# Adding the expert outputs back: four-pass fp32 products with weighted selections, against one-pass products with plain selections and a two-part expert output

## The chip, the cores and the metric

The kernel runs on one core of a Trainium2 chip. Its time is the device time of one execution in microseconds (us); of several executions the median is given. The engines named below are TensorE (PE in the profile, its weight loads PEld), VectorE (DVE), ScalarE (ACT), GpSimd (POOL) and SyncE (SP), which issues nearly all DMAs.

## The reference, cut to what matters

A trunk of two layers over 256 frames of width 1024. Its last part is a mixture of eight experts, of which each frame takes two:

```python
logits = xt.astype(F32) @ w_router.astype(F32)
top_logit, top_idx = lax.top_k(logits, TOP_K)            # TOP_K = 2
gates = jax.nn.softmax(top_logit, axis=-1).reshape(-1)
...
def expert_block(args):
    tok, e = args
    xb = xt[tok]
    return (jax.nn.silu(xb @ w_gate[e]) * (xb @ w_up[e])) @ w_down[e]
...
contrib = y_rows[pos].astype(F32) * gates[:, None]
y = jax.ops.segment_sum(contrib, flat_tok, num_segments=n_tok)
```

What this case is about is the last two lines: each frame gets the rows of its two experts, each times its gate, and this is added to the residual x.

## The kernel before

The first 620 us or so are the two mixers, the dense SwiGLU and the router. After them comes one pass per *item*. An item is one expert with 96 slots for rows (3 groups of 32, `NG` = 3, `GRP` = 32); items 0 to 7 are the eight experts, and up to five more would be run by a loop with a register if an expert had over 96 rows. Each engine has its own program, written out in the order in which it runs; semaphores tie them together (`filled(use)`: TensorE has filled a PSUM bank; `drained(use)`: it has been read).

TensorE's order in an item (`expert_item`, line 1277) is `EXPERT_ORDER`: the first 2048 columns of gate (8 pieces) and up (8), the other 1536 columns of gate and up, then 14 pieces of down. Every piece is a DMA of 1024 KB or 768 KB into a ring that holds 14 of the large ones; SP issues the next one as soon as the piece that lay in its place has been used. The gate, up and down products are plain fp32 on *column* tiles: four products of 32 output rows each, side by side (lines 1203 and 1224). One fp32 product in the code makes two weight loads and two MATMULs in the trace; a product of fp32r operands makes one of each.

The expert's output (32 slots of a group, times 4 quarters `q` of 256 columns, over the 128 partitions) ends in three banks `("md", r)`, numbers 2, 6 and 7. ScalarE copies each to `y_e` (line 1575), and that copy drains the bank.

`one_hot` (VectorE, L1963) writes for each frame and slot whether the frame's row lies in it, times the frame's gate; TensorE turns this over (`turned_selection`, L1239) and ScalarE copies it to `sgt` (L1568). `combine(item)` (L1272) then makes, for each of two frame tiles `t`, three groups `r` and four quarters `q`, one fp32 product of 32 rows with 128 frames and 256 columns: 24 products on *row* tiles, the four quarters in four different row groups of the array, into four banks `("mc", q)`, numbers 3 to 6. VectorE adds these to x, 128x512 at a time (`add_contributions`, L2126), which drains them.

`combine(item - 1)` stands inside the next item, behind gate pieces 0 and 1; seven of the eight stand so. The eighth is the kernel's last work on TensorE, behind the loop with the register, and is followed by `add_contributions`, the final norm and the output.

In the trace `expert_rows` is the memory of `y_e`, `m_silu` and `m_act`, and `arena` that of the selections, `sgt` and the gathered rows.

Of the kernel before, what the change touches and what calls it, by code (L numbers as in the profile page):

```python
# [27 lines left out]
F32 = mybir.dt.float32  # L28
F32R = mybir.dt.float32r
I32 = mybir.dt.int32  # L30
ALU = mybir.AluOpType
ACT = mybir.ActivationFunctionType
AX = mybir.AxisListType.X

P = 128
SEQ = 256
T = SEQ // P
DM = 1024
DK = DM // P
# [8 lines left out]
D_FF = 7 * DM // 2  # L48
FC = 512
NCH = D_FF // FC  # L50
NE = 8
GRP = 32
NG = 3
SLOTS = NG * GRP
NQ = P // GRP
# [193 lines left out]
DN = DM // NQ  # L249
DOWN_ORDER = (2, 0, 1)  # L250
# [100 lines left out]
def build_trunk(nc, x_d, w, cst_d, out_d):  # L351
    uses, bank_fills_per_item, bank_signals_per_item = plan_banks()

    with ExitStack() as ctx:
# [3 lines left out]
        def sem(name):  # L358
            return ctx.enter_context(nc.semaphore(name))
# [12 lines left out]
        def ps(use):  # L372
            return bank[uses[use][0]][:, :]
# [9 lines left out]
        def fill_sem(use):  # L383
            return s_filled[uses[use][0]]

        def drain_sem(use):
            return s_drained[uses[use][0]]

        def open_bank(pe, use, item=0):

            b, n, _ = uses[use]
            if n > 1:
                pe.wait_ge(s_drained[b], n - 1 + item * bank_fills_per_item[b])
# [11 lines left out]
        x = sb("x", [P, T, DM])  # L405
# [45 lines left out]
        def layout(region, *parts):  # L451
            at, out = 0, []
            for shape in parts:
                out.append(view(region, at, *shape))
                at += int(np.prod(shape))
            taken[0] = max(taken[0], at)
            return out
# [14 lines left out]
        ml_h = hn[:, :, 0:512]  # L472
        ml_o = hn[:, :, 512:1024]

        xg_all, xg, m_act_t, sel, sel_q, sgt = layout(
            arena, (NE, DK, SLOTS), (DK, SLOTS), (NG, D_FF // P, GRP), (T, SLOTS), (T, NQ * SLOTS), (NG, SEQ))
        assert taken[0] <= ARENA and T * NE * SLOTS <= NG * D_FF // P * GRP

        xt, xt_parts, w_router = layout(arena, (T, DK, P), (T, P), (DK, GRP))  # L480
        m_silu, m_act, y_e = layout(expert_rows, (NG, 512), (NG, 512), (NG, DN))

        taken[0] = 0
# [79 lines left out]
        rsel_ready = sem("rsel_ready")  # L564
        route_ready = sem("route_ready")
        sel_ready = sem("sel_ready")
        experts_done = sem("experts_done")
        out_ready = sem("out_ready")
        out_done = sem("out_done")
# [209 lines left out]
        def _(pe):  # L779
# [479 lines left out]
            def combine(item):  # L1259

                for r in DOWN_ORDER:
                    pe.wait_ge(*drained(("md", r), item))
                for half in range(2):
                    pe.wait_ge(*drained(("sgt", half), item))
                for t in range(T):
                    for r in range(NG):
                        for q in range(NQ):
                            use = ("mc", q)
                            if t == 0 and r == 0:
                                open_bank(pe, use, item)  # L1270
                            rows = slice(q * GRP, (q + 1) * GRP)
                            last = mm(ps(use)[:, t * DN:(t + 1) * DN], sgt[rows, r, t * P:(t + 1) * P], y_e[rows, r, :],  # L1272
                                      start=r == 0, stop=r == NG - 1)
                            if t == T - 1 and r == NG - 1:
                                last.then_inc(fill_sem(use), 1)

            def expert_item(item, first=False):

# [56 lines left out]
        def _(act):  # L1335
# [223 lines left out]
            def expert_item(item, first=False):  # L1559
                if first:  # L1560
                    for half, k in FIRST_ROWS:
                        gathered_rows(half, k)
                gate_silu(0, item)
                for half in range(2):
                    use = ("sgt", half)
                    act.wait_ge(*filled(use, item))
                    rows = 2 - half
                    fn(sgt[:, 2 * half:2 * half + rows, :],  # L1568
                       ps(use)[:, 0:rows * SEQ].rearrange("p (r c) -> p r c", r=rows), ACT.Copy).then_inc(
                           drain_sem(use), 1)  # L1570
                gate_silu(1, item)
                for r in DOWN_ORDER:
                    use = ("md", r)
                    act.wait_ge(*filled(use, item))
                    fn(y_e[:, r, :], ps(use)[:, 0:DN], ACT.Copy).then_inc(drain_sem(use), 1)  # L1575

            for item in range(NE):
                expert_item(item, item == 0)
# [64 lines left out]
        def _(dve):  # L1643
# [314 lines left out]
            def one_hot(item):  # L1958

                for t in range(T):  # L1960
                    pos = pos_i[:, bass.ds(item, 1), t]
                    slot = cst[:, C_IOTA:C_IOTA + SLOTS].rearrange("p (r s) -> p r s", r=NG)
                    last = V.tensor_scalar(sel_q[:, t, :].rearrange("p (r q s) -> p r q s", r=NG, q=NQ),  # L1963
                                           slot[:, :, None, :].to_broadcast([P, NG, NQ, GRP]), pos,
                                           gate_i[:, bass.ds(item, 1), t], ALU.is_equal, ALU.mult)
                last.then_inc(sel_ready, 1)

            def one_hot_extra(item):
# [134 lines left out]
            def gated(part, item):  # L2103

                width, first = WIDTHS[part], PARTS[part][0] // P
                blocks = width // GRP
                for r in range(NG):
                    use = ("mu", part, r)
                    dve.wait_ge(*drained(("mg", part, r), item))
                    dve.wait_ge(*filled(use, item))  # L2110
                    if part:
                        dve.wait_ge(turned_ready, 2 * NG * item + r + 1)
                    V.tensor_tensor(m_act[:, r, 0:width], m_silu[:, r, 0:width], ps(use)[:, 0:width],  # L2113
                                    ALU.mult).then_inc(drain_sem(use), 1)
                for r in range(NG):
                    dve.wait_ge(*drained(("mu", part, r), item))
                    V.transpose(m_act_t[:, r, first:first + blocks, :].rearrange("p b c -> p (b c)"),
                                m_act[:, r, 0:width]).then_inc(turned_ready, 1)

            def add_contributions(item):  # L2120

                for q in range(NQ):
                    use = ("mc", q)
                    cols = x[:, :, q * DN:(q + 1) * DN]
                    dve.wait_ge(*filled(use, item))
                    V.tensor_tensor(cols, cols, ps(use).rearrange("p (t c) -> p t c", t=T), ALU.add).then_inc(  # L2126
                        drain_sem(use), 1)

            def expert_item(item, first=False):
                if not first:  # L2130
                    add_contributions(item - 1)
                    for half in range(2):
                        dve.wait_ge(*filled(("sgt", half), item - 1))
                one_hot(item)
                gated(0, item)
                gated(1, item)

            def rows_extra(item):

# [45 lines left out]
```

## Time and profile before

| | us |
|---|---|
| three runs of the kernel before | 1520.58, 1522.92, 1525.62 (median 1522.92) |
| the profiled execution | 1522.43 |
| its span in the trace | 1520.6 |
| PE busy | 1458.4 (96% of the span) |
| PEld busy | 892.3 (59%) |
| DVE busy | 410.4 (27%) |
| ACT busy | 328.8 (22%) |
| mean DMA rate over the span | 288 GB/s |

Busy time is what an engine's instructions cover. The chain of waits is read back from the last instruction to what released each step, so that it shows the work that set the end. A windows view gives busy time and the number of instructions that touch each stretch (x), and the granted clock of TensorE (1.00 is 2.4 GHz, 0.50 is 1.2 GHz). Matmuls overlap: the mean of one (from its start to its end) is longer than the distance between two starts.

### The profile page before, as it was taken

The numbers are of one execution on the slowest core, as the hardware profiler recorded it, in microseconds if no ns is written. First come the engines' busy times: TensorE is split into PE (matmuls) and PEld (weight loads), VectorE is DVE, ScalarE is ACT, GpSimd is POOL, SyncE is SP. The second block draws the span as 40 slices with busy tenths as digits, with TensorE's granted clock in tenths as the row PEclk, the third lists the DMA queues.
The fourth block names the chain that finished last, engine by engine and source line by source line (L and its number), as shares of the span: only waits on it lengthen the run. The fifth ranks groups of instructions, "written<-read, shape, count | busy, mean of one in ns | idle before, by whom it ended". The sixth has DMA issues, their size and how long they took to land.

```text
span 1520.6 us, 34140 instructions
## 1 busy us (share of the span) xinstructions
PE 1458.4 (96%) x15653; PEld 892.3 (59%) x15653; DVE 410.4 (27%) x638; ACT 328.8 (22%) x479; POOL 24.5 (2%) x43
## 2 busy tenths in 40 slices
PE   4999899999999979999999999999999999999995
PEld 3986799999798965345345345344344354354353
DVE  3454654444565753300100100100100100000101
ACT  4332544434538642100000000000000000000001
POOL 2000000000001100000000000000000000000000
PEclk9999999999999999999999999999999999999997
DMA  9530555555444328999999999999999999999960
GB/s 308 176 111 28 176 173 191 189 175 191 139 143 149 111 84 318 333 410 403 376 400 400 381 395 399 387 397 391 387 401 389 386 404 392 387 400 392 387 247 29
DMA packets 132600, 438.51 MB, mean 288 GB/s; under 512 B 10626, under 2 KB 63968, under 8 KB 116064
## 3 DMA queue, kind: packets, MB, share of 16 engines
q1 hardware_dynamic: 131232, 432.73, 75.4%
q0 software_dynamic: 1216, 3.51, 0.8%
q8 instruction: 125, 2.05, 0.5%
q14 instruction: 27, 0.22, 0.0%
HBM read 435.16 MB, written 1.05 MB: 287 GB/s over the span
## 4 chain that ended last, share of the span: by engine, by line
PE 93%; DVE 2%; ACT 2%; issue 1%; DMA 1%; SPq 1%; POOL 0%; DVEq 0%; ACTq 0%
PE bank L1203 38%; PE bank L1224 19%; PE bank L799 9%; PE bank L800 9%; PE bank L801 9%; PE bank L1272 2%; ACT high L627 1%; PE bank L1254 1%; PE bank L899 1%; DMA raw<-in_ev_w_in 1%; DVE low L632 1%; PE bank L1239 1%; SPq L740 0%; PE bank L918 0%; PE bank L917 0%
## 5 line engine op out<-in xcount | busy, mean ns | idle before, releaser
L1203 PE MATMUL bank<-ring,arena 128*32 128x512 f32 (+1 forms) x6144 | 585.9, 540 | 0.0
L1203 PEld LDWEIGHTS bank<-ring,arena 128*32 128x32 f32 x6144 | 196.5, 110 | 365.3 <-issue 364.1
L1224 PE MATMUL bank<-ring,arena 128*32 128x256 f32 x5376 | 291.5, 379 | 0.0
L1224 PEld LDWEIGHTS bank<-ring,arena 128*32 128x32 f32 x5376 | 174.7, 110 | 117.1 <-issue 3.1
L632 DVE TENSOR_TENSOR low<-raw,high 128x2048 fp32r<-128x2048 f32 x74 | 169.2, 2290 | 174.7 <-ACT high L627 174.7
L799 PE MATMUL bank<-ht_h,high 128*128 128x256 f32 x672 | 193.7, 288 | 4.0 <-DVE vec L1741 3.0
L800 PE MATMUL bank<-ht_l,high 128*128 128x256 f32 x672 | 192.2, 286 | 0.0
L801 PE MATMUL bank<-ht_h,low 128*128 128x256 f32 x672 | 192.0, 286 | 0.0
L627 ACT ACTIVATE high<-raw 128x2048 fp32r<-128x2048 f32 x74 | 141.6, 1913 | 162.9 <-PE bank L801 159.1
L2113 DVE TENSOR_TENSOR expert_rows<-expert_rows,bank 128x512 f32<-128x512 f32 (+1 forms) x48 | 29.7, 621 | 469.8 <-PE bank L1203 251.2
L799 PEld LDWEIGHTS bank<-ht_h,high 128*128 128x128 f32 x672 | 131.2, 195 | 5.7 <-issue 5.1
L800 PEld LDWEIGHTS bank<-ht_l,high 128*128 128x128 f32 x672 | 131.1, 195 | 0.2
L801 PEld LDWEIGHTS bank<-ht_h,low 128*128 128x128 f32 x672 | 131.1, 195 | 0.0
L2126 DVE TENSOR_TENSOR x<-x,bank 128x512 f32<-128x512 f32 x32 | 19.8, 681 | 341.5 <-PE bank L1272 341.5
L1557 ACT ACTIVATE expert_rows<-bank 128x512 f32<-128x512 f32 (+1 forms) x48 | 25.9, 544 | 351.0 <-PE bank L1203 351.0
L1575 ACT ACTIVATE expert_rows<-bank 128x256 f32<-128x256 f32 x24 | 9.2, 384 | 403.9 <-PE bank L1224 403.9
L799 PE MATMUL bank<-high,ht_h 128*128 128x256 f32 x160 | 46.2, 289 | 0.0
L800 PE MATMUL bank<-low,ht_h 128*128 128x256 f32 x160 | 45.2, 283 | 0.0
L801 PE MATMUL bank<-high,ht_l 128*128 128x256 f32 x160 | 45.2, 283 | 0.0
L800 PE MATMUL bank<-low,f_act_h 128*128 128x512 f32 x112 | 44.7, 399 | 0.0
L799 PE MATMUL bank<-high,f_act_h 128*128 128x512 f32 x112 | 44.1, 394 | 0.0
L801 PE MATMUL bank<-high,f_act_l 128*128 128x512 f32 x112 | 43.9, 392 | 0.0
(289 smaller groups left out, 992.1 us busy)
## 6 DMA issues: line engine op xcount, KB each, us to landing
ring<-in_moe_w_down SPq DMA_DIRECT2D x112, 1024.0 KB, 8.3
ring<-in_moe_w_gate SPq DMA_DIRECT2D x64, 1024.0 KB, 8.9
ring<-in_moe_w_up SPq DMA_DIRECT2D x64, 1024.0 KB, 8.5
ring<-in_moe_w_gate SPq DMA_DIRECT2D x64, 768.0 KB, 5.8
ring<-in_moe_w_up SPq DMA_DIRECT2D x64, 768.0 KB, 6.6
raw<-in_ffn_w_gate SPq DMA_DIRECT2D x14, 1024.0 KB, 5.0
raw<-in_ffn_w_up SPq DMA_DIRECT2D x14, 1024.0 KB, 5.1
raw<-in_ffn_w_down SPq DMA_DIRECT2D x14, 1024.0 KB, 4.9
```

Source lines behind the costliest of these rows:

```text
L627: nc.scalar.activation(high[:, n % SPLITS, :], raw[:, raw_slot(n), :], ACT.Copy).then_inc(high_ready, 1)
L632: nc.vector.tensor_tensor(low[:, n % SPLITS, :], raw[:, raw_slot(n), :], high[:, n % SPLITS, :].bitcast(F32), ALU.subtract).then_inc(split ...
L799: mm(out, l_high, r_high, start=start, stop=False)
L800: mm(out, l_high, r_low, start=False, stop=False)
L801: return mm(out, l_low, r_high, start=False, stop=stop)
L899: mm(o, v[:, 0, h * HD:(h + 1) * HD], q01, start=True, stop=False)
L1203: ins = mm(ps(use)[q * GRP:(q + 1) * GRP, 0:width], rows[:, k, r * GRP:(r + 1) * GRP], weights[:, q, :, :], start=k == 0, stop=k == DK - 1)
L1224: ins = mm(ps(use)[q * GRP:(q + 1) * GRP, 0:DN], m_act_t[:, r, first + c, :], ring[:, at + c * DM + q * DN:at + c * DM + (q + 1) * DN], st ...
L1272: last = mm(ps(use)[:, t * DN:(t + 1) * DN], sgt[rows, r, t * P:(t + 1) * P], y_e[rows, r, :], start=r == 0, stop=r == NG - 1)
L1557: fn(m_silu[:, r, 0:WIDTHS[part]], ps(use)[:, 0:WIDTHS[part]], ACT.Silu).then_inc(drain_sem(use), 1)
L2113: V.tensor_tensor(m_act[:, r, 0:width], m_silu[:, r, 0:width], ps(use)[:, 0:width], ALU.mult).then_inc(drain_sem(use), 1)
L2126: V.tensor_tensor(cols, cols, ps(use).rearrange("p (t c) -> p t c", t=T), ALU.add).then_inc(drain_sem(use), 1)
```

## The change

The selection `sel_q` holds 0 or 1 instead of the gate. `sgt` has the type fp32r. ScalarE copies the expert's output to `y_h` in fp32r (rounded), and a new step on VectorE, `down_low`, writes what is missing, the bank minus `y_h`, to `y_l` in fp32r; this step now drains the bank. `combine` makes each product twice, with `y_h` and with `y_l`, in fp32r. The gate is applied where VectorE adds to x: one instruction per quarter and frame tile, with the gate as a scalar of each partition.

```diff
+        y_h = nc.alloc_sbuf_tensor_at("y_h", [P, NG, DN], F32R, offset=ht_at + 2 * NG * 512 * 4)
+        y_l = nc.alloc_sbuf_tensor_at("y_l", [P, NG, DN], F32R, offset=ht_at)
...
 def combine(item):
                 for t in range(T):
                     for r in range(NG):
-                        for q in range(NQ):
-                            use = ("mc", q)
-                            if t == 0 and r == 0:
-                                open_bank(pe, use, item)
-                            rows = slice(q * GRP, (q + 1) * GRP)
-                            last = mm(ps(use)[:, t * DN:(t + 1) * DN], sgt[rows, r, t * P:(t + 1) * P], y_e[rows, r, :],
-                                      start=r == 0, stop=r == NG - 1)
+                        for part in (y_h, y_l):
+                            first, final = r == 0 and part is y_h, r == NG - 1 and part is y_l
+                            for q in range(NQ):
+                                use = ("mc", q)
+                                if t == 0 and first:
+                                    open_bank(pe, use, item)
+                                rows = slice(q * GRP, (q + 1) * GRP)
+                                last = mm(ps(use)[:, t * DN:(t + 1) * DN], sgt[rows, r, t * P:(t + 1) * P],
+                                          part[rows, r, :], start=first, stop=final)
...
-                    fn(y_e[:, r, :], ps(use)[:, 0:DN], ACT.Copy).then_inc(drain_sem(use), 1)
+                    fn(y_h[:, r, :], ps(use)[:, 0:DN], ACT.Copy).then_inc(y_high, 1)
...
-                                           slot[:, :, None, :].to_broadcast([P, NG, NQ, GRP]), pos,
-                                           gate_i[:, bass.ds(item, 1), t], ALU.is_equal, ALU.mult)
+                                           slot[:, :, None, :].to_broadcast([P, NG, NQ, GRP]), pos, None,
+                                           ALU.is_equal)
...
+            def down_low(item):
+                for n, r in enumerate(DOWN_ORDER):
+                    use = ("md", r)
+                    dve.wait_ge(y_high, NG * item + n + 1)
+                    V.tensor_tensor(y_l[:, r, :], ps(use)[:, 0:DN], y_h[:, r, :].bitcast(F32), ALU.subtract).then_inc(
+                        drain_sem(use), 1)
+
+            def gated_rows(item, q, t):
+                cols = x[:, t, q * DN:(q + 1) * DN]
+                return V.scalar_tensor_tensor(cols, ps(("mc", q))[:, t * DN:(t + 1) * DN],
+                                              gate_i[:, bass.ds(item, 1), t], cols, ALU.mult, ALU.add)
...
 def add_contributions(item):
-                    V.tensor_tensor(cols, cols, ps(use).rearrange("p (t c) -> p t c", t=T), ALU.add).then_inc(
-                        drain_sem(use), 1)
+                    for t in range(T):
+                        last = gated_rows(item, q, t)
+                    last.then_inc(drain_sem(use), 1)
...
                 gated(1, item)
+                down_low(item)
```

On TensorE, at the `combine` of item 0 (inside item 1), before:

```order
3545 L1203 MATMUL bank<-ring,arena 32x512 x11
3546 L1272 MATMUL bank<-expert_rows,arena 128x256 [waits drained7,drained3,drained6,drained2]
3547 L1272 MATMUL bank<-expert_rows,arena 128x256 [waits drained4]
3548 L1272 MATMUL bank<-expert_rows,arena 128x256 [waits drained5]
3549 L1272 MATMUL bank<-expert_rows,arena 128x256 [waits drained6]
3550 L1272 MATMUL bank<-expert_rows,arena 128x256 x20
3551 L1203 MATMUL bank<-ring,arena 32x512 [waits expert_full2]
```

and now (line 1279 is the product in the changed file):

```order
3546 L1279 MATMUL bank<-y_h,sgt 128x256 [waits drained7,drained3,drained6,drained2]
3547 L1279 MATMUL bank<-y_h,sgt 128x256 [waits drained4]
3548 L1279 MATMUL bank<-y_h,sgt 128x256 [waits drained5]
3549 L1279 MATMUL bank<-y_h,sgt 128x256 [waits drained6]
3550 L1279 MATMUL bank<-y_l,sgt 128x256 x4
3551 L1279 MATMUL bank<-y_h,sgt 128x256 x4
3552 L1279 MATMUL bank<-y_l,sgt 128x256 x4
```

The block stays at the same place with the same waits; 24 products have become 48, in fours of `y_h` and `y_l` by turns.

On VectorE, between the end of item 0's gated rows and the next item's selection, before:

```order
435 L2117 STREAM_TRANSPOSE arena<-expert_rows 128x384 [waits drained3]
436 L2117 STREAM_TRANSPOSE arena<-expert_rows 128x384 [waits drained4]
437 L2117 STREAM_TRANSPOSE arena<-expert_rows 128x384 [waits drained5]
438 L2126 TENSOR_TENSOR x<-x,bank 128x2x256 [waits filled3]
439 L2126 TENSOR_TENSOR x<-x,bank 128x2x256 [waits filled4]
440 L2126 TENSOR_TENSOR x<-x,bank 128x2x256 [waits filled5]
441 L2126 TENSOR_TENSOR x<-x,bank 128x2x256 [waits filled6]
442 L1963 TENSOR_SCALAR arena<-cst,s_cols 128x384 [waits filled7]
```

and now (`s_cols` holds the gates):

```order
437 L2124 STREAM_TRANSPOSE arena<-expert_rows 128x384 [waits drained5]
438 L2132 TENSOR_TENSOR y_l<-bank,y_h 128x256 [waits y_high] x3
439 L2138 SCALAR_TENSOR_TENSOR x<-bank,s_cols,x 128x256 [waits filled3]
440 L2138 SCALAR_TENSOR_TENSOR x<-bank,s_cols,x 128x256
441 L2138 SCALAR_TENSOR_TENSOR x<-bank,s_cols,x 128x256 [waits filled4]
442 L2138 SCALAR_TENSOR_TENSOR x<-bank,s_cols,x 128x256
443 L2138 SCALAR_TENSOR_TENSOR x<-bank,s_cols,x 128x256 [waits filled5]
444 L2138 SCALAR_TENSOR_TENSOR x<-bank,s_cols,x 128x256
445 L2138 SCALAR_TENSOR_TENSOR x<-bank,s_cols,x 128x256 [waits filled6]
446 L2138 SCALAR_TENSOR_TENSOR x<-bank,s_cols,x 128x256
```

Three subtractions have come in that wait for ScalarE, and four additions of 512 columns have become eight of 256 with a scalar.

## Rows read from the trace of the kernel before

**Rows 1.** The page, part 4: the chain's shares by engine.

```profile
PE 93%; DVE 2%; ACT 2%; issue 1%; DMA 1%; SPq 1%; POOL 0%; DVEq 0%; ACTq 0%
```

**Rows 2.** The chain, 700 us to the end: start us, us, what.

```profile
714.06 2.80 PE bank L1272 x48
...
821.50 5.15 PE bank L1203 x48
826.65 2.80 PE bank L1272 x48
...
1389.62 2.80 PE bank L1272 x48
...
1497.60 6.99 issue
```

**Rows 3.** DMAs and loads by windows: us, PE, PEld, DVE, ACT, POOL, clock, DMA, GB/s.

```profile
1465.00:1470.00 5.00, 5.00 (x100) 3.02 (x96) 0.00 (x0) 0.00 (x0) 0.00 (x0) 1.00 0.70 277
1470.00:1475.00 5.00, 5.00 (x100) 3.02 (x96) 0.00 (x0) 0.00 (x0) 0.00 (x0) 1.00 0.03 7
```

**Rows 4.** Timeline of PE around one combine: start us, us, what.

```profile
826.58 2.87 PE L1272 MATMUL bank<-expert_rows,arena 32*128 32x256 f32 x48
```

**Rows 5.** L1272 as a source line, whole run: duration min/median/max in ns.

```profile
L1272 PE MATMUL bank<-expert_rows,arena x384: 374/374/791, 714.0 to 1509.6; 32*128 32x256 f32 x192
```

**Rows 6.** L1272 in windows of 0.02 us: us, PE busy (x), PEld busy (x).

```profile
826.58:826.60 0.02, 0.02 (x3) 0.02 (x3) 1.00 0.00 0
...
826.70:826.72 0.02, 0.02 (x4) 0.02 (x8) 1.00 0.98 410
...
826.90:826.92 0.02, 0.02 (x7) 0.01 (x3) 1.00 0.00 0
```

**Rows 7.** Timeline of the dense SwiGLU, fp32r on the whole array.

```profile
330.34 0.19 PEld L799 LDWEIGHTS bank<-ht_h,high 128*128 128x128 f32 x1
...
330.45 0.28 PE L799 MATMUL bank<-ht_h,high 128*128 128x256 f32 x1
...
330.57 0.28 PE L800 MATMUL bank<-ht_l,high 128*128 128x256 f32 x1
```

**Rows 8.** L1164 (small column tiles) in windows of 0.05 us.

```profile
576.05:576.10 0.05, 0.05 (x12) 0.05 (x8) 1.00 2.41 492
```

**Rows 9.** Timeline of the tail.

```profile
1497.21 0.38 ACT L1575 ACTIVATE expert_rows<-bank 128x256 f32<-128x256 f32 x1 [0.48 <-PE bank L1224]
1500.16 1.28 ACT L1584 ACT_TABLE_LOAD   x1 [2.57 <-issue]
...
1504.59 5.45 PE L1272 MATMUL bank<-expert_rows,arena 32*128 32x256 f32 x48 [7.53 <-issue]
1510.01 2.48 DVE L2126 TENSOR_TENSOR x<-x,bank 128x512 f32<-128x512 f32 x4 [47.05 <-PE bank L1272]
```

**Rows 10.** Clock in the tail, by windows as in the third group.

```profile
1504.50:1507.00 2.50, 2.41 (x21) 2.41 (x25) 0.00 (x0) 0.00 (x0) 0.00 (x0) 0.50 0.00 0
```

**Rows 11.** DVE by line and shape: busy us, mean ns, idle before.

```profile
L1810 DVE TENSOR_TENSOR f_act_l<-arena,f_act_h 128x256 fp32r<-128x256 f32 x28 | 10.5, 418 | 0.0
L1752 DVE SCALAR_TENSOR_TENSOR arena<-bank,s_cols,cst 128x256 f32<-128x256 f32 x12 | 5.7, 474 | 0.0
L1865 DVE SCALAR_TENSOR_TENSOR arena<-mq_in,vec,arena 128x254 f32<-128x254 f32 x4 | 2.3, 574 | 0.1
```

**Rows 12.** Timeline of DVE in the first mixer: start us, us, what.

```profile
96.86 0.35 DVE L1750 SCALAR_TENSOR_TENSOR arena<-bank,s_cols,cst 128x128 f32<-128x128 f32 x1
97.12 0.48 DVE L1752 SCALAR_TENSOR_TENSOR arena<-bank,s_cols,cst 128x256 f32<-128x256 f32 x1
```

**Rows 13.** Timeline of ACT at an item's end.

```profile
819.92 0.38 ACT L1575 ACTIVATE expert_rows<-bank 128x256 f32<-128x256 f32 x1 [49.52 <-PE bank L1224]
...
821.65 0.38 ACT L1575 ACTIVATE expert_rows<-bank 128x256 f32<-128x256 f32 x1 [0.48 <-PE bank L1224]
```

More of the change, by code:

```diff
@@ L473, in build_trunk @@
         ml_o = hn[:, :, 512:1024]
-        xg_all, xg, m_act_t, sel, sel_q, sgt = layout(
+        xg_all, xg, m_act_t, sel, sel_q, _ = layout(
             arena, (NE, DK, SLOTS), (DK, SLOTS), (NG, D_FF // P, GRP), (T, SLOTS), (T, NQ * SLOTS), (NG, SEQ))
+        sgt = nc.alloc_sbuf_tensor_at("sgt", [P, NG, SEQ], F32R, offset=arena_at + 4 * (
+            (NE + 1) * DK * SLOTS + NG * D_FF // P * GRP + T * SLOTS + T * NQ * SLOTS))
         assert taken[0] <= ARENA and T * NE * SLOTS <= NG * D_FF // P * GRP
         xt, xt_parts, w_router = layout(arena, (T, DK, P), (T, P), (DK, GRP))
-        m_silu, m_act, y_e = layout(expert_rows, (NG, 512), (NG, 512), (NG, DN))
+        m_silu, m_act = layout(expert_rows, (NG, 512), (NG, 512))
+        y_h = nc.alloc_sbuf_tensor_at("y_h", [P, NG, DN], F32R, offset=ht_at + 2 * NG * 512 * 4)
+        y_l = nc.alloc_sbuf_tensor_at("y_l", [P, NG, DN], F32R, offset=ht_at)
         taken[0] = 0
@@ L566, in build_trunk @@
         sel_ready = sem("sel_ready")
+        y_high = sem("y_high")
         experts_done = sem("experts_done")
@@ L1266, in combine @@
                     for r in range(NG):
-                        for q in range(NQ):
-                            use = ("mc", q)
-                            if t == 0 and r == 0:
-                                open_bank(pe, use, item)
-                            rows = slice(q * GRP, (q + 1) * GRP)
-                            last = mm(ps(use)[:, t * DN:(t + 1) * DN], sgt[rows, r, t * P:(t + 1) * P], y_e[rows, r, :],
-                                      start=r == 0, stop=r == NG - 1)
-                            if t == T - 1 and r == NG - 1:
-                                last.then_inc(fill_sem(use), 1)
+                        for part in (y_h, y_l):
[7 more added lines that the diff above has]
+                                          part[rows, r, :], start=first, stop=final)
+                                if t == T - 1 and final:
+                                    last.then_inc(fill_sem(use), 1)
             def expert_item(item, first=False):
@@ L2123, in add_contributions @@
                     use = ("mc", q)
-                    cols = x[:, :, q * DN:(q + 1) * DN]
                     dve.wait_ge(*filled(use, item))
-                    V.tensor_tensor(cols, cols, ps(use).rearrange("p (t c) -> p t c", t=T), ALU.add).then_inc(
-                        drain_sem(use), 1)
+                    for t in range(T):
+                        last = gated_rows(item, q, t)
+                    last.then_inc(drain_sem(use), 1)
             def expert_item(item, first=False):
```

## The prediction

> **What bounds the kernel now.** I read the chain of waits first, then TensorE's timeline at one combine, then the windows inside it, and at last the tail. The reader is to see in the chain that 93% of the span is TensorE's own work [rows 1], and in its list by time that the item phase is TensorE alone: from one combine to the next (714.06, 826.65) are 112.6 us, and between the pieces stands no other engine and no DMA, up to the seventh combine at 1389.62 [rows 2]. So a microsecond taken out of TensorE there comes off the time, seven times over, provided that DMAs and banks keep up.
>
> That the DMAs keep up is read at the end of their work. The windows show 277 GB/s from 1465 to 1470 us and 7 GB/s after it [rows 3], while TensorE goes on with down pieces until 1497.6 [rows 2]. The last piece therefore lay in the ring some 27 us before it was used up. If the DMAs did not speed up at all, seven shorter combines would eat under 10 of these 27 us.
>
> The eighth combine is on the path too, in another state: TensorE issues nothing for 6.99 us behind the last down piece (it runs the loop with the register) [rows 2], then combine takes 5.45 us [rows 9], at a granted clock of 0.50, which is 1.2 GHz [rows 10], against 2.87 us at full clock [rows 4]. Behind it VectorE adds to x for 2.48 us with TensorE idle [rows 9].
>
> **The change part by part.**
>
> *Combine, seven times at full clock.* Before, one takes 2.87 us from its first start to its last end [rows 4]. It is 48 MATMULs in 12 sets of four, one for each row group. The windows show how they run: three or four start within 0.02 us, so the four row groups work side by side, and the next set starts at 826.90, 0.32 us behind the first at 826.58 [rows 6]. With 0.37 us for the last set's own MATMULs (the line's median [rows 5]), the ten distances in between are (2.87 - 0.32 - 0.37)/10 = 0.218 us. A MATMUL of fp32r of the same 256 columns starts 0.12 us behind the one before it (330.45, 330.57) and lasts 0.28 us [rows 7]. The fp32 set of 0.218 us is thus two passes per MATMUL of about 0.107 us (256 columns at 2.4 GHz) and about 0.005 us over; an fp32r set is one pass. The new combine has again 48 MATMULs in 12 sets: first distance 0.32 - 0.107 = 0.21, ten distances between 0.112 (one pass and the same 0.005) and 0.12 us (the pair on the whole array), the last MATMUL 0.28 us. With 0.115 that is 0.21 + 1.15 + 0.28 = 1.64 us, so 1.23 us less; 1.18 to 1.26 at the ends. Seven of them: 8.6 us (8.3 to 8.8).
>
> Can TensorE issue that fast? A pair of weight load and MATMUL would have to start every 0.029 us, and in the combine of before it is 0.055. In the router's small products 12 MATMULs of about 0.27 us are in flight at once beside 8 weight loads [rows 8], which is one start per 0.023 us. So it can, at least for 16 pairs in a row. Seen from the other side: if the distance could not fall below today's, nothing would be gained; I keep that as a rival.
>
> Here a rule speaks against the change. The Trainium skill, "TensorE: Matmul & The Clock Gate", Part 3 (The mechanism), says that a weight load overlaps with running MATMULs only where its row group is another one. By that rule, a row group would load, then multiply, then load; each set of the new combine would cost a load and a pass, about what two passes cost now, and the gain would be nil. This case's trace does not agree: on the whole array, where every load has the same rows as the MATMUL before it, a load of 0.19 us starts at 330.34 and yet the MATMULs follow each other at 0.12 us [rows 7]; and eight loads run at once beside the first four MATMULs of a combine [rows 6].
>
> *The eighth combine, at 1.2 GHz.* It stands behind the same idle time, so I take the same clock. 12 sets lose one pass each of 256/1.2 GHz = 0.213 us: 2.56 us less, 2.9 us instead of 5.45. Bounds: 2.3 to 2.8 us, since loads too are slower there.
>
> *Rounding and the low part.* ScalarE's three copies keep form and place. VectorE gets three subtractions of 128x256 from a bank, about 0.42 us each (the dense SwiGLU's low parts take 418 ns) [rows 11]. Each begins when ScalarE's copy ends: the copies start at 819.92 and 821.65 for the first and the last bank [rows 13]. The first bank (number 2) is wanted again by the third product group of the next item's first piece, about 821.50 + 2 x 0.86 = 823.2 (a group of eight MATMULs of that line takes 5.15/6 = 0.86 us [rows 2]); it will be free by 819.92 + 0.38 + 0.1 + 0.42 = 820.8. The last one is free at 822.6, and combine starts at 826.58. VectorE has nothing else there. Cost nil, with 2.4 and 4 us of cover. Behind the last item the cover is TensorE's 6.99 us.
>
> *Adding with the gate.* Eight SCALAR_TENSOR_TENSOR of 128x256 with a scalar take the place of four TENSOR_TENSOR of 128x512. The nearest row has a bank, a scalar and a second tensor: 474 ns, and the one ahead of it shows a distance to the next start 0.09 us under its own duration (97.12 - 96.86 = 0.26 against 0.35) [rows 11, 12]. Eight: 7 x 0.385 + 0.475 = 3.17 us, +0.7 us over the 2.48. The upper bound is the 574 ns row [rows 11]: 7 x 0.485 + 0.574 = 3.97 us, +1.5; the lower is none. In the seven inner items this is covered: the banks are wanted again by up piece 0, six gate pieces (some 15 us) behind combine. Queued behind the additions on VectorE is the next selection, which TensorE wants at that same place. In the tail it is on the path, so it costs 0.7 us once. VectorE now also enters its register loop only after the last low part, near 1498.2 instead of near 1463. ScalarE needs 2.57 us for its own such loop and TensorE 6.99 [rows 2, 9]; by the longer one VectorE is ready at 1505.2, and combine will end at 1504.6 + 2.9 = 1507.5. Nil, with 2 us of cover.
>
> *The selection without the gate* does less work on VectorE, beside TensorE. Nil.
>
> **Sum.** -8.6 - 2.56 + 0.7 = -10.5 us, made against the profiled execution of 1522.43 us (span 1520.6). That is 1512.0 us. The median shown, 1522.92, is 0.5 us above that execution, so the sum goes for it as it stands. With all ends: -8.3 - 2.3 + 1.5 = -9.1 and -8.8 - 2.8 + 0 = -11.6, or 1510.8 to 1513.3; the three runs shown lie 5 us apart, so the likeliest case's own range is 1509 to 1516.
>
> **The rivals.**
>
> *Sets overlap only in part* (banks or operand reads of four one-pass products get in each other's way). For: never seen here at one start per 0.029 us for 48 in a row. Against: the fp32 passes too write four banks at once, at full rate. By a distance of 0.16 us, halfway from 0.107 to today's: combine 2.1 us, saving 0.77 x 7 = 5.4, the eighth perhaps 2, +0.7: -6.7, 1515.7 us. In the same part of the skill four row tiles of 32 rows and 512 columns are given as 3.07 times faster than one after another, not 4; that is an estimate of 4 x 0.12/3.07 = 0.156 us per set, near this rival; the fp32 sets of before, at full rate, don't agree with it.
>
> *No gain on TensorE* (the distance is set by loads or issue, 0.218 us as now; this is also what the skill's rule above would do). For: 48 loads in both cases. Against: the loads and starts in [rows 7, 8]. Then only the tail's +0.7 remains: 1523.1 us.
>
> **How the numbers follow.** The forecast has 0.72, partial overlap 0.10, no gain 0.08, one after another 0.08, and 0.02 is for a wait that I didn't see. About 0.3% (4.6 us) is what a measurement of this kernel can tell from no change. Faster by more than that: 0.72 and nearly all of the 0.10, with a little off for noise, 0.83; within: 0.09; slower: 0.08. The range takes in the forecast with its bounds and the partial overlap: 1508.5 to 1518.
>
> **What would show it.** Right: in the profile after, the list by time has 48 MATMULs of combine in 1.6 to 1.7 us (2.80 in the chain of before), at distances of 111.4 us from one to the next; 12 or more of them in flight in a window of 0.05 us; the eighth near 2.9 us; eight additions in 3.2 us at the end; ring and banks never a releaser of TensorE. A combine of 2.1, 2.8 or near 6 us names its rival. The forecast is wrong beyond that if TensorE waits for VectorE's low part at an item's start, if the idle time ahead of the eighth combine grows, or if VectorE starts to add later than TensorE ends.

## The result, and the profile after

The changed kernel takes 1513.2 us in the median of five runs (1511.04 to 1515.33) against 1522.92 us before (five runs, 1519.78 to 1525.62): 9.7 us less, a ratio of 0.9941 (95% interval 0.9922 to 0.996). Forecast were 1512.0 us and -10.5 us. A second comparison, on another occasion, gave 1512.81 against 1522.71 us, 0.993 (0.9917 to 0.9943).

The chain by time of the changed kernel, start us, us, what, answers to [rows 2]:

```profile
716.29 1.64 PE bank L1279 x35
...
822.57 5.15 PE bank L1208 x48
827.72 1.63 PE bank L1279 x38
...
1384.82 1.63 PE bank L1279 x37
...
1492.08 6.18 issue
1498.27 2.96 PE bank L1279 x41
```

From one combine to the next are now 111.42 us, where it was 112.59: 1.17 us less, seven times. TensorE's timeline inside one combine shows the twelve sets (answers to [rows 4]):

```profile
827.65 0.40 PE L1279 MATMUL bank<-y_h,sgt 32*128 32x256 f32 x4
827.87 0.28 PE L1279 MATMUL bank<-y_l,sgt 32*128 32x256 f32 x4
827.99 0.28 PE L1279 MATMUL bank<-y_h,sgt 32*128 32x256 f32 x4
...
829.07 0.28 PE L1279 MATMUL bank<-y_l,sgt 32*128 32x256 f32 x4
```

Four products start together, and the next four 0.12 us later. In a window of 0.05 us (us, PE busy (x), PEld busy (x)) twelve products and eight weight loads are at work in the changed kernel (first line); in the kernel before, such a window inside a combine has eight products (second line):

```profile
828.35:828.40 0.05, 0.05 (x12) 0.05 (x8) 1.00 0.79 328
```

```profile
828.35:828.40 0.05, 0.05 (x8) 0.05 (x4) 1.00 2.00 819
```

The end of the kernel, as timeline and as windows (us, PE, PEld, DVE, ACT, POOL, clock, DMA, GB/s), answers to [rows 9, 10]:

```profile
1491.65 0.42 DVE L2132 TENSOR_TENSOR y_l<-bank,y_h 128x256 fp32r<-128x256 f32 x1 [0.44 <-ACT y_h L1582]
...
1498.27 0.81 PE L1279 MATMUL bank<-y_h,sgt 32*128 32x256 f32 x4 [7.18 <-issue]
...
1500.80 0.62 PE L1279 MATMUL bank<-y_l,sgt 32*128 32x256 f32 x4
1501.39 3.23 DVE L2138 SCALAR_TENSOR_TENSOR x<-bank,s_cols,x 128x256 f32<-128x256 f32 x8 [9.32 <-PE bank L1279]
```

```profile
1494.00:1498.20 4.20, 0.00 (x0) 0.00 (x0) 0.00 (x0) 1.49 (x2) 0.00 (x0) 0.61 0.02 4
1498.20:1501.40 3.20, 3.13 (x48) 2.86 (x48) 0.01 (x1) 0.00 (x0) 0.00 (x0) 0.50 0.00 0
```

The low part is ready at 1492.07, and TensorE still does nothing until 1498.27; its clock falls meanwhile, and the eighth combine takes 1500.80 + 0.62 - 1498.27 = 3.15 us instead of 5.45. The eight additions take 3.23 us instead of 2.48. The last DMA of weights lands about 26 us before the last down piece is used up, as in [rows 3]:

```profile
1460.00:1465.00 5.00, 5.00 (x97) 2.99 (x92) 0.00 (x0) 0.00 (x0) 0.00 (x0) 1.00 0.48 189
1465.00:1470.00 5.00, 5.00 (x100) 3.02 (x96) 0.00 (x0) 0.00 (x0) 0.00 (x0) 1.00 0.02 7
```

**Reading two spans that differ by something else.** The spans of the two profiled executions are 1520.6 and 1512.7 us, only 7.9 apart. The first combine starts at 714.06 before and at 716.29 after, with the same products ahead of it. The router's gathering (its first product at 582.0 and 584.2) shows the same 2.2 us already, so they arise ahead of it. The windows of 120 to 200 us show part of where: the granted clock was 0.98 in one execution and 0.90 in the other (before, then after):

```profile
120.00:200.00 80.00, 75.32 (x468) 63.33 (x464) 41.59 (x72) 34.06 (x62) 0.54 (x1) 0.98 0.31 103
```

```profile
120.00:200.00 80.00, 75.98 (x422) 62.66 (x421) 38.75 (x68) 32.11 (x58) 0.54 (x1) 0.90 0.28 94
```

What the change touches begins at the first combine. From there to the end of the span it is 1520.6 - 714.06 = 806.5 us before and 1512.7 - 716.29 = 796.4 us after: -10.1 us. I use this stretch below as a second measure beside the ratio; the changed kernel profiled once more had 1513.8 - 717.54 = 796.3 us.

### The profile page after: what moved, and what is told of

Same layout as the page of the kernel before. It is cut to its first block, busy times and chain, and to the rows that moved or that the text cites. A ratio compares the mean times of both kernels' runs of the same rounds, so it can differ in the third digit from the quotient of the medians.

```text
span 1512.7 us, 34198 instructions
## 1 busy us (share of the span) xinstructions
PE 1451.0 (96%) x15653; PEld 886.6 (59%) x15653; DVE 426.0 (28%) x694; ACT 328.9 (22%) x479; POOL 24.6 (2%) x43
## 4 chain that ended last, share of the span: by engine, by line
PE 92%; DVE 3%; ACT 2%; issue 1%; DMA 1%; SPq 1%; POOL 0%; DVEq 0%; ACTq 0%
PE bank L1208 39%; PE bank L1229 19%; PE bank L804 9%; PE bank L805 9%; PE bank L806 9%; ACT high L632 1%; PE bank L1279 1%; PE bank L1259 1%; PE bank L904 1%; DMA raw<-in_ev_w_in 1%; DVE low L637 1%; PE bank L1244 1%; SPq L745 0%; PE bank L923 0%; PE bank L922 0%
## 5 line engine op out<-in xcount | busy, mean ns | idle before, releaser
L1582 ACT ACTIVATE y_h<-bank 128x256 fp32r<-128x256 f32 x24 | 9.2, 384 | 403.8 <-PE bank L1229 403.8
L2132 DVE TENSOR_TENSOR y_l<-bank,y_h 128x256 fp32r<-128x256 f32 x24 | 10.2, 425 | 270.5 <-ACT y_h L1582 270.5
```

## The experiments

Timed runs stand beside the kernel before on the same chip. Line numbers are those of the variant.

**Gate and selections alone (e1).** The products stay fp32 and single:

```diff
-        sgt = nc.alloc_sbuf_tensor_at("sgt", [P, NG, SEQ], F32R, ...
+        sgt = nc.alloc_sbuf_tensor_at("sgt", [P, NG, SEQ], F32, ...
-        y_h = nc.alloc_sbuf_tensor_at("y_h", [P, NG, DN], F32R, ...
+        y_h = nc.alloc_sbuf_tensor_at("y_h", [P, NG, DN], F32, ...
-                        for part in (y_h, y_l):
-                            first, final = r == 0 and part is y_h, r == NG - 1 and part is y_l
+                        for part in (y_h,):
+                            first, final = r == 0, r == NG - 1
...
-                    fn(y_h[:, r, :], ps(use)[:, 0:DN], ACT.Copy).then_inc(y_high, 1)
+                    fn(y_h[:, r, :], ps(use)[:, 0:DN], ACT.Copy).then_inc(drain_sem(use), 1)
...
-                down_low(item)
```

> One part of the change alone: selections of 0 and 1 and the gate applied when VectorE adds to x, but combine as in the kernel before: 24 plain fp32 products, one copy of the expert output, no low part. Theory (all of the gain is TensorE's passes; the gated additions cost only behind the last combine): combine 2.87 us in the items and 5.4 us at the end, the eight last additions 3.2 us instead of 2.5, so +0.7 us against the kernel before, about 1523.6 us. Rival (part of the gain comes from VectorE's new form or from the selection without gate): below 1521 us.

Measured: 1523.41 us (12 runs) against 1522.73 (17 runs), ratio 1.0009 (1.0000 to 1.0018), so +0.7 us. The chain by time:

```profile
825.24 2.80 PE bank L1279 x48
937.83 2.80 PE bank L1279 x48
...
1503.05 5.46 PE bank L1279 x45
```

and VectorE's last additions:

```profile
1508.67 3.23 DVE L2138 SCALAR_TENSOR_TENSOR x<-bank,s_cols,x 128x256 f32<-128x256 f32 x8 [47.12 <-PE bank L1279]
```

The distance stays at 112.59 us. The gated additions cost 0.75 us behind the last combine (3.23 against 2.48) and nothing in the seven inner items; none of the gain is VectorE's.

**High part alone (e2).** The changed kernel with 24 fp32r products instead of 48; the output lacks the low part:

```diff
-                        for part in (y_h, y_l):
-                            first, final = r == 0 and part is y_h, r == NG - 1 and part is y_l
+                        for part in (y_h,):
+                            first, final = r == 0, r == NG - 1
...
-                    fn(y_h[:, r, :], ps(use)[:, 0:DN], ACT.Copy).then_inc(y_high, 1)
+                    fn(y_h[:, r, :], ps(use)[:, 0:DN], ACT.Copy).then_inc(drain_sem(use), 1)
...
-                down_low(item)
```

> The changed kernel without the low part: combine adds the rounded high part alone (24 fp32r products in 6 sets), and the three subtractions are gone. Theory (a set of four fp32r products costs one pass, 0.112 us at full clock and 0.213 us at half clock): combine 0.21 + 4 x 0.112 + 0.27 = 0.93 us instead of 1.63, seven times 0.7 is 4.9 us, and 1.3 us at the end, so 6.2 us under the changed kernel, near 1507 us. Rival (the new combine is bound by something that does not grow with the number of sets, as the switch between tilings): combine stays above 1.3 us and the kernel above 1510 us.

Measured: 1506.38 us against 1522.73, ratio 0.989 (0.9874 to 0.9907; five runs). The chain by time:

```profile
825.03 0.91 PE bank L1279 x18
...
1491.46 1.65 PE bank L1279 x19
```

Six sets fewer take 1.63 - 0.91 = 0.72 us off at full clock, 0.12 a set, and 2.96 - 1.65 = 1.31 us at half clock, 0.218 a set. So the new combine grows with its sets, by little more than the 0.107 us that one pass was worked out to take; the low part costs 7 x 0.72 + 1.31 = 6.35 us of the time.

**Six in a row in one row group (e3).** The same 48 products in another order:

```diff
                 for t in range(T):
-                    for r in range(NG):
-                        for part in (y_h, y_l):
-                            for q in range(NQ):
+                    for q in range(NQ):
+                        for r in range(NG):
+                            for part in (y_h, y_l):
```

> The same 48 fp32r products in another order: quarter by quarter, so that six in a row lie in the same row group of the array. Theory (fp32r products of different row groups run side by side, those of one group one after another at the distance of the whole array, 0.112 to 0.12 us): combine about 48 x 0.115 + 0.3 = 5.8 us instead of 1.63, +4.2 us seven times, and at half clock 48 x 0.213 + 0.4 = 10.6 instead of 2.96 at the end, less some 2.4 us because the first quarters can be added while TensorE works on the last: about +35 us, near 1548 us. Rival (the skill's rule that a weight load overlaps with running products only of another row group): load and pass follow each other, about 0.21 us a product, combine 10 us, about +70 us. Rival (they were never side by side): combine stays at 1.63 us.

Measured: one run, 1523.8 us; the expectation of 1548 us was wrong. Combine takes 3.33 us and not 5.8. The eighth, at half clock, runs from 1506.44 to 1511.87 + 0.41, which is 5.84 us and not 10.6; VectorE adds its first quarters meanwhile. The chain, then the last line of the timeline of TensorE:

```profile
825.89 3.33 PE bank L1279 x42
```

```profile
1511.87 0.41 PE L1279 MATMUL bank<-y_l,sgt 32*128 32x256 f32 x1
```

The timeline of an inner combine shows why:

```profile
825.82 0.38 PE L1279 MATMUL bank<-y_h,sgt 32*128 32x256 f32 x1
826.04 0.27 PE L1279 MATMUL bank<-y_l,sgt 32*128 32x256 f32 x1
826.16 0.38 PE L1279 MATMUL bank<-y_h,sgt 32*128 32x256 f32 x2
826.28 0.39 PE L1279 MATMUL bank<-y_l,sgt 32*128 32x256 f32 x2
826.40 0.49 PE L1279 MATMUL bank<-y_h,sgt 32*128 32x256 f32 x3
```

From the third start on two products run at once, and a little later three, though six products of one row group stand ahead of the first of the next in the program. A line of this view holds every product of one form that begins before the one ahead of it ends: the three of the line at 826.40 start at 826.40, 826.50 and 826.51. So the third row group comes in with the sixth start of the first. TensorE does not start the products in the program's order. It does slow down (3.33 against 1.63 us, distance 113.11 against 111.42), so the order by quarter inside each pair of r and part is worth 1.7 us an item; but it is not the price of having no overlap at all, which this run did not produce.

**Twelve in a row (e10),** to tell two explanations of e3 apart:

```diff
-                for t in range(T):
-                    for r in range(NG):
-                        for part in (y_h, y_l):
-                            for q in range(NQ):
+                for q in range(NQ):
+                    for t in range(T):
+                        for r in range(NG):
+                            for part in (y_h, y_l):
```

> The changed kernel with the 48 products of combine ordered by quarter first, so that twelve in a row lie in one row group (six in the earlier run, in which combine took 3.33 us and three row groups ran side by side although six products of one stood ahead of the first of the next). Theory A (TensorE looks ahead over a fixed number of instructions and starts products of a free row group out of order): with twelve in a row it reaches only one group further, two run side by side, and combine takes about 24 x 0.115 + some 0.5 = 3.5 to 4.5 us. Theory B (each row group has a queue of its own, with no common depth): as with six, about 3.3 us or less. Theory C (strict order of starts): 4 x 11 x 0.115 + 0.3 = 5.4 us, and then the earlier run cannot be explained.

Measured: one run, 1553.59 us, 40 us over the changed kernel. Combine takes 4.82 us in some items, up to 5.77 in others:

```profile
716.74 5.48 PE bank L1278 x48
722.22 20.74 PE bank L1208 x168
...
834.58 4.82 PE bank L1278 x48
839.40 18.16 PE bank L1208 x168
```

In the timeline of the combine at 834.5 eight products start alone, and from the ninth on there are two:

```profile
835.45 0.28 PE L1278 MATMUL bank<-y_l,sgt 32*128 32x256 f32 x1
835.58 0.38 PE L1278 MATMUL bank<-y_h,sgt 32*128 32x256 f32 x2
```

With six in a row the seventh product starts with the third; with twelve the thirteenth starts with the ninth. Both times it goes off together with the product four places ahead of it, while the three between wait for their row group. In e3 the same holds once more: the thirteenth product, the first of the third row group, starts with the ninth (826.51 and 826.50). That is what theory A says, a common lookahead, and it reaches four products in both runs; theory B would have given at least the three groups of e3, and strict order (5.4 us) is refuted by e3. The time of 4.82 us is above the 3.5 to 4.5 that I had worked out for A, since only the last four of twelve overlap. Seven times 4.82 - 1.63 = 3.19 us are 22.3 of the 38.7 us that lie between the two kernels from the first combine on. The clock is another 13: in six of the seven inner items combine itself, the 168 products of line 1208 behind it, or both took longer (5.48 instead of 4.82 us, and 20.74 instead of 18.16 us, in the first). The end, with an eighth combine of 8.57 us, is the last 3. The windows of the first item show

```profile
716.00:722.20 6.20, 6.20 (x60) 5.31 (x56) 2.63 (x6) 0.00 (x0) 0.00 (x0) 0.87 1.00 415
722.20:725.00 2.80, 2.80 (x17) 0.74 (x20) 1.92 (x4) 0.00 (x0) 0.00 (x0) 0.50 0.30 123
```

TensorE had no pause, one or two row groups worked in combine, and the granted clock fell to 0.50. The item whose combine starts at 834.58 had the same products and no fall; what spares it, no view shows. In e3 all seven inner combines took 3.33 to 3.35 us at a distance of 113.11 us, and in the windows over each of them and what follows the clock is 1.00.

**The low part later (e4, e5).** Two or eight more copies on VectorE ahead of each subtraction, in items 0 to 7:

```diff
                     dve.wait_ge(y_high, NG * item + n + 1)
+                    for _ in range(2 if isinstance(item, int) else 0):        # e5: 8
+                        steps.done(V.tensor_copy(view(expert_rows, 3840, 256), ps(use)[:, 0:DN]))
```

> The changed kernel, with two more copies of 128x256 on VectorE (into memory that nobody reads) ahead of each subtraction of the low part, in items 0 to 7: the low part comes 1 us later for the first bank and about 2 us later for the last. Theory (the low part is covered by 2.4 us at the first bank and 4 us at the last, and by TensorE's 7 us at the end): no wait on TensorE, distance from one combine to the next unchanged at 111.42 us. Rival (some of it is already on the path, by a wait that the profile puts down to something else): the distance grows by about 1 us an item, +8 us in all.

> As the run with two more copies, but with eight ahead of each subtraction (about 0.48 us each): the first bank is free some 3.9 us later, the last some 11.5 us later. Theory (covers of 2.4 and 4 us): TensorE waits about 1.5 us for the first bank in the next item's first piece and then for the last bank at combine; combine starts some 7 us later than without the copies, the distance from one combine to the next is near 118.3 us instead of 111.42, and the end comes some 5 us later: about +53 us. Rival (the cover is larger than I worked out, or none): distance near 111.4, or near 123 us.

Measured with two copies: one run, 1512.32 us. The low part of the last bank comes 1.7 us later behind ScalarE's copy (2.53 us from the copy's start to its end, where the changed kernel has 0.85), and the chain by time has the distance unchanged, to 0.01 us:

```profile
825.18 1.64 PE bank L1279 x41
936.61 1.64 PE bank L1279 x41
```

With eight: one run, 1570.98 us, distance 119.49 us. The low part of the last bank comes 9.9 us later, not 11.5, and TensorE waits twice: for the first bank in the next item's first piece, and for the last one ahead of combine. Timeline (start us, us, what), chain by time, then windows:

```profile
829.35 3.64 PE L1208 MATMUL bank<-ring,arena 128*32 128x512 f32 x32 [1.27 <-DVE y_l L2134]
...
836.87 0.42 DVE L2134 TENSOR_TENSOR y_l<-bank,y_h 128x256 fp32r<-128x256 f32 x1
837.50 0.58 PE L1279 MATMUL bank<-y_h,sgt 32*128 32x256 f32 x4 [4.51 <-issue]
```

```profile
837.50 2.93 PE bank L1279 x43
840.44 18.95 PE bank L1208 x168
```

```profile
837.50:840.00 2.50, 2.50 (x45) 2.50 (x48) 0.00 (x0) 0.00 (x0) 0.00 (x0) 0.50 0.30 118
```

The profile puts the second wait down to "issue", but combine starts 0.2 us behind the end of the last low part (836.87 + 0.42). The cover is real and finite: 1.7 us of delay cost nothing, 9.9 us cost 8.1 us an item. Of these, 1.27 + 4.51 = 5.8 us are idle time, where I had 6.9 because I had made the delay too long; with the delays measured, 3.7 us at the first bank and 9.9 at the last, the covers come out at 2.4 and 4.1 us, as worked out. Another 2.1 us are the clock, which I had left out: combine ran at half clock (2.93 instead of 1.63 us), and so did part of the 168 products behind it (18.95 instead of 18.16 us), after TensorE had stood still. A wait that is worked out only as idle time is priced too low.

**One branch around the loop (e6), number of items read earlier (e7).** On TensorE, and likewise on ScalarE and VectorE:

```diff
+                if item == NE - 1:                                       # e7 alone
+                    n_items = pe.value_load(route_i[0:1, 0:1], ...)      # e7 alone
...
-            with pe.Fori(NE, NITEM) as item:
-                with pe.If(n_items > item):
+            with pe.If(n_items > NE):
+                with pe.Fori(NE, NITEM) as item:
+                    with pe.If(n_items > item):
```

> The changed kernel with one branch around the loop for extra items on TensorE, ScalarE and VectorE, so that the loop's five turns are skipped at once where no expert has over 96 rows. Theory (TensorE's 7 us without work ahead of the last combine are mostly the five turns, and they also let its clock fall to 1.2 GHz): the idle time falls to about 3 us, combine starts near 1494.5 instead of 1498.3 and takes 1.7 us instead of 2.96 if the clock stays up: 4 to 5.5 us less than the changed kernel, near 1508.5 us. Rival (the idle time is the read of the number of items from memory, not the turns): less than 1 us gained.

> As the run with one branch, and the three engines read the number of items ahead of the last expert instead of behind it. Theory: the read is then hidden behind queued products, and combine starts as soon as the low part is there (1492.1) or a branch's time after it: 5.5 to 7.5 us less than the changed kernel, near 1506.5 us. Rival (the read stops TensorE wherever it stands): same time as with one branch alone, and an idle stretch ahead of the last expert.

Measured: e6 1508.93 us, ratio 0.9913 (0.9896 to 0.9929); e7 1508.4 us, 0.9905 (0.989 to 0.9921), both against 1522.71 (six runs each). From the first combine to the end 1507.4 - 714.51 = 792.9 and 1507.4 - 714.44 = 793.0 us, some 3.4 less than the changed kernel. The chain of e6:

```profile
1493.02 2.83 PE bank L1279 x45
```

and e7's timeline:

```profile
1489.78 1.28 ACT L1595 ACT_TABLE_LOAD   x1
...
1493.00 0.69 PE L1279 MATMUL bank<-y_h,sgt 32*128 32x256 f32 x4 [3.77 <-issue]
```

The turns of the loop were 3.4 us of TensorE's 7. ScalarE waited 2.57 us in the changed kernel, 0.53 us with the branch alone, and goes on at once with the early read. TensorE does not gain by that read, it still starts 3.77 us late: e7's expectation was wrong. And the clock still fell, so combine took 2.8 to 2.9 us and not 1.7. What TensorE does in these 3.8 us (the jump over its long loop body is my guess) no view of the engines shows. The DMA view has a hint: in e6's stretch from 1489.3 to 1493.02 one packet of 16 KB of instructions moves on queue q8 (kind, packets, MB, share of 16 engines); the changed kernel moves two there in its 7 us:

```profile
q8 instruction: 1, 0.02, 1.8%
```

That fits a jump that waits for code, but it does not show that TensorE waited for this packet.

**The eighth combine ahead of the branch (e8).**

```diff
             for item in range(1, NE):
                 ...
                 expert_item(item)
+            combine(NE - 1)
...
                         gather_extra(item)
                         expert_item(item)
-            combine(n_items - 1)
+                        combine(item)
```

and the same with `add_contributions` on VectorE.

> As the run with the early read of the number of items and one branch, and the eighth combine and its additions stand ahead of the branch, directly behind the last down piece, with constants in their waits; the loop for extra items adds its own items at their end. Theory (TensorE's 3.7 us ahead of the last combine in that run are the jump over its long loop body, and its clock falls in them): combine waits for the low part alone, starts about 0.9 us behind the last down piece instead of 3.7, and runs at full clock in 1.65 us instead of 2.9; the additions end some 6.4 us behind the last down piece instead of 10: 3.5 us less than the run with the early read, 7 us less than the changed kernel, near 1505.5 us. Rival (VectorE's and ScalarE's own jump now lies on the path and takes what was saved): no faster than 1508 us.

Measured: 1506.52 us (four runs) against 1522.59, ratio 0.99 (0.9884 to 0.9917): 16 us under the kernel before, and below the changed kernel's 1512.81 and 1513.2. From the first combine to the end 1501.3 - 712.30 = 789.0 us, 7.4 less than the changed kernel (7 expected). Chain, windows and timeline:

```profile
1488.28 1.69 PE bank L1279 x44
```

```profile
1488.30:1490.00 1.70, 1.69 (x48) 1.48 (x48) 0.00 (x1) 0.82 (x2) 0.00 (x0) 1.00 0.00 0
```

```profile
1488.28 0.39 PE L1279 MATMUL bank<-y_h,sgt 32*128 32x256 f32 x4 [1.19 <-issue]
...
1490.00 3.23 DVE L2143 SCALAR_TENSOR_TENSOR x<-bank,s_cols,x 128x256 f32<-128x256 f32 x8 [1.92 <-PE bank L1279]
```

Now the low part is on the path (TensorE idles 1.19 us, of which ScalarE's copy and the subtraction are 0.83), the clock stays at 1.00, the eighth combine costs about what the others do (1.69 against 1.63 us), and no packet of instructions moves in the idle time. This run moves the code and saves the jump in one step, so it shows what the place behind the branch costs and not which part of the jump costs it.

**The changed kernel again.**

> The changed kernel once more, beside the others on the same chip. Expected: 0.994 of the kernel before, as in the first comparison; and, in the trace, the same distance of 111.42 us from one combine to the next, while the time of the first combine differs by some us from run to run (714.06 us in the profile before, 716.29 in that after), because the noise lies in the stages ahead of the items.

Measured 0.993 (0.9917 to 0.9943); distance 111.42 us; first combine at 717.54 us. In the eleven profiles in which nothing holds it up (all but e5) it lies between 712.30 and 717.54 us, while from it to the end the two profiles of the changed kernel differ by 0.1 us. Most of the noise of this kernel is ahead of the items.

## Why the prediction was right, point by point

Right in sign, size and mechanism: 1513.2 us against 1512.0, inside the likeliest case's own range.

- *Combine at full clock*: forecast 1.64 us from first start to last end, measured 829.07 + 0.28 - 827.65 = 1.70. The term was off in one number, the distance between sets: I took 0.115 us, it is 0.12, the whole array's pair distance [rows 7] and my upper end. Seven times -1.17 us is -8.2 instead of -8.6. That the passes are the price is shown by e2 (0.12 us a set), and that nothing else gained by e1.
- *The eighth combine*: forecast 2.9, measured 3.15 us. The sets are 0.213 us apart as worked out; the first set and the last product's own 0.62 us were longer than I had left for them.
- *Low part*: no cost, as forecast; e4 shows that there were 1.7 us to spare, e5 that there were not 9.9, and its two waits give the covers of 2.4 and 4 us that I had worked out. In the tail it hid behind TensorE's own 7 us; e8 shows the price when that cover is gone, most of 1.2 us of waiting.
- *Additions with the gate*: forecast +0.7 us once, measured +0.75 (3.23 against 2.48), and +0.7 in e1.
- *Idle time ahead of the eighth combine*: 7.53 us before [rows 9], 7.18 after, which is -0.35 that I had not forecast and do not explain.
- *The rate of issue*: I read one start per 0.023 us out of [rows 8], as if the twelve products in flight had started evenly over one product's 0.27 us. The fours there start 0.11 to 0.13 us apart (at 575.83, 575.97, 576.08 and 576.19), so a start per 0.028 to 0.033 us. The conclusion held, since the changed kernel starts one per 0.03 us, but the row gave it no margin.
- Sum from the first combine on: -8.2 - 2.3 + 0.75 - 0.35 = -10.1, as measured. That it comes so near to the -10.5 is in part luck: 0.7 us too much in the combines stands against 0.35 us of idle time that was not in the sum.

Of the rivals, *partial overlap* and *no gain on TensorE* fell with the set distance of 0.12 us. *Not side by side* fell with four simultaneous starts; the experiment meant to show its price (e3) could not, because TensorE overlaps row groups even when the program does not ask for it. That price stays an argument; e10 with 4.82 us, two groups at most, is the nearest measurement. The Trainium skill's rule that I weighed ("TensorE: Matmul & The Clock Gate", Part 3, The mechanism: loads overlap with running products of another row group only) does not hold here: a load takes 0.18 us and a product 0.28 us, and yet the sets follow at 0.12 us with each group's next load inside.

## What to carry to other kernels

Where TensorE alone is on the path, count passes: a plain fp32 product on row tiles cost four passes and two fp32r products cost two (2.80 against 1.63 us for a combine), so splitting one operand in two fp32r parts took 0.58 of the time, as long as the other operand is exact (zeros and ones here), and what has to be multiplied in can go to an engine that waits anyway. Price an idle stretch of TensorE with the half clock that can follow it (it did behind 3.7 us and more, in e5 to e7 and the changed kernel, and did not behind the 1.19 us of e8), and put the last products ahead of a branch or loop, not behind it. When two profiles differ by a few microseconds, first find the place from which they should differ, and compare from there.

## What the runs showed of the hardware that I had not expected

- TensorE starts a product of a free row group ahead of three earlier ones of a busy group (e3, e10). The Trainium skill, "TensorE: Matmul & The Clock Gate", Part 3 (The mechanism), says that matmuls start in strict program order; these two timelines do not agree.
- With one or two row groups at work in a combine and no pause, the granted clock fell to 0.50 in six of seven items (e10); with mostly three (e3) or four (the changed kernel) it stayed at 1.00 in all seven.
- The first combine's start varied by 5.2 us between executions of nearly the same code ahead of it, with different granted clocks in the first mixer.
